# Softmax rows of the second attention on GpSimd, and longer lags in the second and the long attention

## The reference

```
# first block
A: diff_attention        4 heads, two softmaxes per head, p0 - lam * p1
B: chunk_band_attention  8 heads of 64:  sc = q k^T * d**-0.5 + rel_table ; softmax ; p @ v
C: memory_attention      4 heads of 128 over 256 memory tokens: softmax ; p @ v
# second block
N: nsa_mixer, 16 heads in 4 groups; per block of 128 queries three branches
   o_c : softmax over 31 compressed keys        ("c" rows, 4 x 32 wide)
   o_s : softmax over the selected keys         ("s" rows)
   o_w : softmax over a window of keys          ("w" rows)
   out = g0 * o_c + g1 * o_s + g2 * o_w         (g = sigmoid gates)
X: cross_attention, 4 heads of 64 over 256 memory tokens
```

## Time and profile before

| | |
|---|---|
| runs, median (lowest to highest) | 2284.83 us (2282.06 to 2284.85) |
| profiled execution, its own time | 2282.84 us |
| its span | 2280.3 us, mean granted TensorE clock 0.994 |
| PE busy | 2238.8 us (98%) |
| DVE, ACT, POOL busy | 1179.0 (52%), 964.5 (42%), 229.5 us (10%) |
| second attention (B, C) | 624.6 to 684.1 us of the span |
| long attention (N, X) | 1583.4 to 1774.1 us of the span |

### The profile page before, as it was taken

The page is one execution under the profiler, slowest core; times in us unless marked ns, Lnnn a source line. Parts: engine busy times, 40 slices in busy tenths (PEclk is TensorE's granted clock), DMA queues, the critical chain, the costliest instruction groups (busy, mean ns, idle before and its releaser), DMA issues.

```text
span 2280.3 us, 29997 instructions
## 1 busy us (share of the span) xinstructions
PE 2238.8 (98%) x11038; PEld 1797.9 (79%) x11038; DVE 1179.0 (52%) x2092; ACT 964.5 (42%) x1582; POOL 229.5 (10%) x247
## 2 busy tenths in 40 slices
PE   8999999999999999999999999999999999999998
PEld 6888888877868888888888887787566788888887
DVE  7434436675475556434435656754666554432432
ACT  7332223456585333332223422634788434322322
POOL 2000001100210001000001420000443001000011
PEclk9999999999999999999999999999999999999999
DMA  6322322311302232322332382232000132332331
GB/s 244 111 87 86 113 94 80 111 56 56 111 11 92 83 110 95 109 92 83 104 108 69 103 255 72 68 96 74 2 2 34 60 111 93 110 92 92 96 107 55
DMA packets 213646, 206.81 MB, mean 91 GB/s; under 512 B 4880, under 2 KB 194576, under 8 KB 213296
## 3 DMA queue, kind: packets, MB, share of 16 engines
q1 hardware_dynamic: 210544, 192.31, 26.8%
q0 software_dynamic: 3008, 13.24, 1.8%
HBM read 199.25 MB, written 4.19 MB: 89 GB/s over the span
## 4 chain that ended last, share of the span: by engine, by line
PE 90%; DVE 5%; ACT 2%; issue 2%; DMA 1%; POOL 0%; SPq 0%; ACTq 0%; DVEq 0%; POOLq 0%
PE ps L906 26%; PE ps L908 26%; PE ps L907 26%; PE ps L705 3%; PE ps L732 2%; PE ps L1138 2%; DMA wraw<-in_w_in 1%; DVE Sm L855 1%; PE ps L1047 1%; PE ps L1178 1%; DVE wlo L571 1%; PE ps L1203 1%; ACT whi L564 0%; ACT Sm L803 0%; PE ps L1157 0%
## 5 line engine op out<-in xcount | busy, mean ns | idle before, releaser
L906 PE MATMUL ps<-hH,whi 128*128 128x512 f32 x1528 | 601.1, 393 | 2.2 <-DVE wlo L571 2.2
L908 PE MATMUL ps<-hH,wlo 128*128 128x512 f32 x1528 | 594.7, 389 | 0.0
L907 PE MATMUL ps<-hL,whi 128*128 128x512 f32 x1528 | 594.6, 389 | 0.0
L571 DVE TENSOR_TENSOR wlo<-wraw,whi 128x2048 fp32r<-128x2048 f32 x192 | 441.3, 2299 | 285.8 <-ACT whi L564 285.8
L564 ACT ACTIVATE whi<-wraw 128x2048 fp32r<-128x2048 f32 x192 | 367.0, 1911 | 504.5 <-PE ps L908 494.9
L906 PEld LDWEIGHTS ps<-hH,whi 128*128 128x128 f32 x1528 | 286.3, 187 | 66.1 <-issue 3.3
L907 PEld LDWEIGHTS ps<-hL,whi 128*128 128x128 f32 x1528 | 286.3, 187 | 62.5 <-issue 3.1
L908 PEld LDWEIGHTS ps<-hH,wlo 128*128 128x128 f32 x1528 | 286.3, 187 | 60.4
L906 PE MATMUL ps<-gH,whi 128*128 128x512 f32 x608 | 237.2, 390 | 0.0
L908 PE MATMUL ps<-gH,wlo 128*128 128x512 f32 x608 | 236.6, 389 | 0.0
L907 PE MATMUL ps<-gL,whi 128*128 128x512 f32 x608 | 236.6, 389 | 0.0
(11 more groups left out here) (376 smaller groups left out, 2674.1 us busy)
## 6 DMA issues: line engine op xcount, KB each, us to landing
wraw<-in_w_in SPq DMA_DIRECT2D x45, 1024.0 KB, 5.1
wraw<-in_ffn_wg SPq DMA_DIRECT2D x22, 1024.0 KB, 5.2
wraw<-in_ffn_wu SPq DMA_DIRECT2D x22, 1024.0 KB, 5.1
wraw<-in_w_up SPq DMA_DIRECT2D x16, 1024.0 KB, 5.2
wraw<-in_w_down SPq DMA_DIRECT2D x16, 1024.0 KB, 5.7
wraw<-in_ffn_wd SPq DMA_DIRECT2D x16, 768.0 KB, 4.6
wraw<-in_w_gate SPq DMA_DIRECT2D x12, 1024.0 KB, 4.9
wraw<-in_ffn_wd SPq DMA_DIRECT2D x16, 640.0 KB, 4.3
```

The source lines that it names most:

```text
L571: dve.tensor_tensor(wlo[s][:, :], wraw[s][:, :], f32(whi[s][:, :]), ALU.subtract).then_inc(w_lo[s], 1)
L906: pe.matmul(o, lh, rh, start=start, stop=False)
L907: pe.matmul(o, lh, rl, start=False, stop=False)
L908: return pe.matmul(o, ll, rh, start=False, stop=stop)
```

## The change

Lags: A stays at 6, N and X go from 4 to 6, B and C from 3 to 4. Rings: A stays at 8 buffers, N and X have 7, B and C still 5. Since a ring is now shorter than the lag would need, VectorE gets a wait: before it writes the row of step k (not in A) it waits until the row that used the buffer (k-7 or k-5) was transposed (`t_full`). The multiplication of all 48 rows of B and C moves from VectorE to GpSimd, in a form without a gate; X stays on VectorE, and so do the c rows. GpSimd therefore runs `pool_attention` for B and C too. The bias jobs of heads 0 to 3 stay ahead of it; the last four jobs (mask added for heads 4 to 7, and two loads) are put behind its rows 7, 9, 15 and 17. The semaphore counts of N start at 48.

```diff
         def lag_of(kind):
-            return 6 if kind == "A" else 4 if kind in "NX" else 3
+            return 6 if kind in "ANX" else 4
...
-                ring = SmB if kind in "BC" else Sm[0:lag_of(kind) + 2]
-                self.Sm = ring[k % len(ring)]
+                ring = SmB if kind in "BC" else Sm[0:8 if kind == "A" else 7]
+                self.Sm, self.rows = ring[k % len(ring)], len(ring)
...
-            by_pool = 0
+            by_pool = 48 if names[0] == "N0" else 0
             for e in seq:
-                on_pool = e.kind == "N" and e.m != "c"
+                on_pool = e.kind in "BCN" and e.m != "c"
...
-        def pool_attention(pool, names):
-            for e in steps(names)[0]:
+        def pool_attention(pool, names, behind={}):
+            for k, e in enumerate(steps(names)[0]):
                 if not e.p:
                     continue
                 pool.wait_ge(s_recip, e.p)
-                pool.tensor_scalar(e.Sm[:, 0:e.n], e.Sm[:, 0:e.n], st[:, 16 + e.s % 8:17 + e.s % 8], gate_of(e),
-                                   ALU.mult, ALU.mult).then_inc(s_pool, 1)
+                r_ = st[:, 16 + e.s % 8:17 + e.s % 8]
+                if e.kind == "N":
+                    pool.tensor_scalar(e.Sm[:, 0:e.n], e.Sm[:, 0:e.n], r_, gate_of(e), ALU.mult, ALU.mult).then_inc(s_pool, 1)
+                else:
+                    pool.tensor_scalar(e.Sm[:, 0:e.n], e.Sm[:, 0:e.n], r_, None, ALU.mult).then_inc(s_pool, 1)
+                if k in behind:
+                    behind[k]()
...
-            if lag == 4:
-                for slot in range(0, len(seq) + 4, 2):
+            if names[0] == "N0":
+                for slot in range(0, len(seq) + lag, 2):
                     scores_from(slot)
-                    turns_from(slot - 4)
-                    values_from(slot - 6, 2)
+                    turns_from(slot - lag)
+                    values_from(slot - lag - 2, 2)
...
                     dve.wait_ge(s_full, e.s + 1)
+                    if e.kind != "A" and slot >= e.rows:
+                        dve.wait_ge(t_full, seq[slot - e.rows].u + 1)
...
-            for h in range(8 + 2):
+            def bias_of(h):
                 if h >= 2:
                     b = bias4[(h - 2) % 4]
...
+            for h in range(6):
+                bias_of(h)
+            pool_attention(pool, ["B", "C"], {7: lambda: bias_of(6), 9: lambda: bias_of(7), 15: lambda: bias_of(8), 17: lambda: bias_of(9)})
             pool_squares(pool, NORM["ffn2"])
```

## The result

The changed kernel takes 2297.06 us (median of 4 runs, 2296.33 to 2301.19); the kernel before, run beside it, 2284.49 (2282.06 to 2284.85). The ratio is 1.0067, 95% interval 1.0055 to 1.0079: slower by 0.67%, against a forecast of 2280.0 and a range that ended at 2286.5. Both stages lost. First the chain of the page (answers to the earlier trace rows), then the windows of the two stages (answer to the earlier trace rows).

What follows compares the result with a forecast made beforehand. TensorE, busy 98% of the span, was taken as the bound. The second attention's -2.6 us and the long attention's -2.2 gave -4.8, from 2284.83 to 2280.0 us, range 2273 to 2286.5.

Steps and rivals of the forecast that it cites:

- GpSimd's row: Second attention: a row on GpSimd costs 0.45 to 0.77 us, on average 0.8 with the step between, against TensorE's 1.24.
- The sum for B and C: Second attention, all terms: -2.4 - 3.5 + 2.5 + 1.0 - 0.2 = -2.6 us, between -6.1 and +3.
- The lag alone: Second attention: transpositions side by side -2.4 us, ScalarE's copies behind later exponentials +1.0, the end -0.2.
- The multiplication with the bias jobs behind it: Second attention: multiplication leaving VectorE -3.5 us, rows waiting behind bias jobs in GpSimd's queue +2.5 (0 to 7.8).
- VectorE's stretched rows: Second attention: VectorE's multiplications, stretched while GpSimd adds a bias mask, go; their gaps with tails are 3.5 us.
- The long attention's -0.8 a round: Long attention: lag 6 shortens TensorE's gaps by 0.8 us a round, -3.2 over four rounds (0 to -8).
- gap said to go: Long attention: gaps before 1650.55 (a copy, -0.5 us) and before 1674.22 (the c row, -0.4) vanish at lag 6.
- The fill: Start of the long attention: later first transposition and copies, longer stretch at clock 0.50, +1.5 us (0 to +4).
- The new wait: Long attention: VectorE waiting for a transposition before writing an odd step's row costs 0, unless TensorE is held there.
- ring is too short: Rival, both attentions: a transposition held by a copy also holds VectorE's odd steps; +7.1 us, 2291.9, chance 0.10.
- locked out: Rival: GpSimd's rows hold up VectorE's masks, 0.25 x 48 = +12 us, less the 4.8: 2292, chance 0.03.
- Elastic: Rival: longer lag lets TensorE work ahead, half of N's idle time goes (-6), -11.1 us, 2273.7, chance 0.24.

Runs made afterwards that it cites:

- e2: Against the kernel before, only the long attention changed (lag 6, seven row buffers, the wait): 2292.77 us, ratio 1.0052.
- e3: Against the kernel before, only the second attention changed, GpSimd's rows written with two multiplications, by the reciprocal and a column of ones: ratio 0.9987.
- e8: Against the kernel before, only the second attention changed, GpSimd's rows multiplied by the reciprocal and the constant 1.0: ratio 0.9987, second attention 55.9 us.
- e7: Against the kernel before, second attention at lag 4 with transpositions side by side, multiplication left on VectorE: ratio 0.9998, second attention 58.6 us.
- e11: Against the kernel before, long attention at lag 6 with seven buffers and the wait, values spread one row per pair ahead of transpositions: 2279.85 us, ratio 0.9987.
- e4: Against the kernel before, only the long attention changed, lag 6 with eight row buffers and no wait: ratio 1.0042, round 44.6 us.
- e1: Against the kernel before, only the second attention changed (rows on GpSimd without a gate, lag 4): 2287.50 us, ratio 1.0026.

## Why the prediction was wrong

The forecast was -2.6 us for the second attention and -2.2 for the long one; measured were +4.4 and +11.1 (+9.4 in e2, without the round of 46.4). One step failed in each.

- *GpSimd's row (the step that failed in the second attention).* "A row costs 0.45 to 0.77 us ... It keeps up." Those rows are of the form with a gate. Of the form that the change adds no row was on the trace, and I took the two for one instruction. It costs 0.60 to 1.56 us. By the counts by width the 48 rows take 8 x 0.60 + 24 x 0.92 + 8 x 1.24 + 8 x 1.56 = 49.3 us, and with the bias jobs GpSimd is busy for 54.9 of 63.9 us. It doesn't keep up, and twelve idle times of TensorE end with its rows. The form alone is worth 63.9 - 55.9 = 8.0 us. An operation that the trace does not show had to be bounded, and was not.
- *The sum for B and C* was -2.6. With the form put right it is -3.3 (e3) to -3.6 (e8). That it comes so near is in part luck, as its terms err both ways. The lag alone was to bring -2.4 + 1.0 (copies) - 0.2 = -1.6 and brought -0.9 (e7); the copies do take back about 1 us, as forecast (1.26 in three gaps). The multiplication with the bias jobs behind it was to bring -3.5 + 2.5 = -1.0 and brought -2.7; the jobs leave one printed gap of 0.2 to 0.3, not 2.5. The upper bound was added up wrongly: with the bounds given it is +3.7, not +3.
- *The rule of the Trainium skill*, page "GPSIMD Engine Reference", section "Engine selection": an input of one tensor is "roughly line-rate". In e8 it comes near (0.69 against VectorE's 0.49 in the earlier trace rows, 1.4 times); the changed kernel's form takes 1.56, three times VectorE's. The measurement decides: the rule does not hold for that form.
- *VectorE's stretched rows.* That they go with the multiplication was right. In e7, where VectorE still multiplies, they are there again; its VectorE, and its GpSimd at that time:

```profile
631.11 1.83 DVE L899 TENSOR_SCALAR Sm<-Sm,st 128x512 f32<-128x512 f32 x1
```

```profile
631.37 1.28 POOL L1237 TENSOR_TENSOR bias<-bias_raw,cst 128x512 f32<-128x512 f32 x1
```

  The Trainium skill's page "SBUF — State Buffer", section "Who interferes with whom", says that VectorE and GpSimd share a pair of ports and that either can block the other. The runs agree as far as VectorE is slow where the addition runs; the multiplication shown is stretched although it began 0.26 us before the addition, the addition takes 1.27 us with or without it, and nothing here isolates the port.
- *The long attention's -0.8 a round (the step that failed there)* was +2.6. "I asked of each gap which exponential stands ahead of the copy" looked at one gap at a time with the rest held still. Neither gap said to go went: the wait for the c row is 0.37 at 1727.89 (0.30 before), and the one at the first 512-wide pair hides in the group at 1702.61. Others came in, at 1695.14 and 1718.04, where the run of values now falls behind another pair; with the values spread (e11) they are gone. The premise, that the gaps are of the copy's order only, missed what makes the copy late: scores issued after a lump. That is 1.5 of the 2.6; for the other 1.1 no step can be named.
- *The fill*, +1.5: c values start 13.4 us after the first scores, 11.6 before: +1.8. The size is right. The longer stretch at clock 0.50 that was part of it isn't there: about 6.4 us in the changed kernel's profile, 9.9 before and 10.3 in e2, whose fill is as long. What is there is two new waits of TensorE for VectorE's c steps, 1.33 and 1.02 us.
- *The new wait, 0*: 0.2 a round at most (e4). Nearly right. The slow rival "ring is too short" named the right sign for the wrong cause, and "locked out" did not happen: the masks of 512 columns take 0.69 us as before.
- *Elastic* assumed that a longer lag lets TensorE work ahead. In this kernel it cannot: by the waits for the banks it issues scores at most four steps ahead of the masks, whatever the lag, and transposes at most two rows ahead of the copies.

## What to carry to other kernels

A duration belongs to a form of an instruction, its number of operations included: before an operation is moved to another engine, look for a row of exactly that form there, and where none is, bound it widely. In a pipeline over several engines, the longest stretch in which the feeding engine issues nothing for the others can count more than how far apart its stages stand. Here spreading that work evenly, with its place moved ahead of the transpositions, was worth 1.5 us of a 42 us round at lag 4 and 3.0 of 45 at lag 6, while a lag of 6 or 8 without it cost 2.6 or 1.9.

## What the runs showed of the hardware

- GpSimd multiplies a float32 row of 128 partitions by one scalar in 0.60, 0.92, 1.24, 1.56 us (128, 256, 384, 512 columns); by a scalar and a constant 1.0 in 0.37, 0.48, 0.58, 0.69; by two scalars from memory in 0.45, 0.56, 0.66, 0.77. So the form with more arithmetic is the quicker one. Why was not tried.
- The masks of VectorE take 0.69 us for 512 columns beside such rows as without them, while its multiplications of 512 columns take up to 1.84 beside an addition on GpSimd and 0.49 without it.
- The same idle times can stand before a fall of the granted clock or not. In the second round of the changed kernel TensorE waited 0.37 and 0.73 us from 1681.1 on, the clock went from 1.00 to 0.50, the 1.2 GHz level, near 1683 and was back at 1.00 at 1687; the round ran at 0.96 and took 46.4 us. One round later the same two waits stand (1727.89 and 1729.21), the clock stays at 1.00 and the round takes 44.8. The second attention of e1 ran at 0.95 in one execution and at 1.00 in another.
